# Norm sums by a matrix of ones, roots of whole rows, and buffers of its own for the second feed-forward unit

## The reference

```
def rms_norm(x, g):
    return x * rsqrt(mean(x*x, axis=-1) + 1e-6) * g
for l in range(2):                                   # first model
    mixed = mixer_l(rms_norm(h, norm_mix_pre[l])) @ w_out[l]       # recurrence / window attention, memory attention
    h = h + rms_norm(mixed, norm_mix_post[l])
    f = (silu(g) * u) @ w_ffn_out[l]                 # g, u = halves of rms_norm(h, norm_ffn_pre[l]) @ w_ffn_in[l]
    h = h + rms_norm(f, norm_ffn_post[l])
    if l == 0:
        kv = rms_norm(h, norm_kv) @ w_kv_shared
# second model: x + position, modulated norm, mLSTM and Fourier mixer, w_out_2,
# x = x + gate1 * rmsnorm(y); router on 16 experts; x + gate2 * rmsnorm(moe)
```

## Time and profile before

| what | value |
|---|---|
| median of 3 runs | 1950.71 us |
| lowest, highest | 1950.61, 1956.45 us |
| span of the profiled execution, first to last instruction | 1947.3 us |
| own time of that execution | not recorded beside its span |
| mean granted TensorE clock | 0.950 |
| TensorE busy | 1814.3 us |
| VectorE busy | 1216.2 us |
| ScalarE busy | 896.1 us |

### The profile page before, as it was taken

How to read it: one execution, slowest core, us unless ns; L and a number is a source line. 1 busy time by engine, 2 the same in 40 slices (tenths; PEclk the granted TensorE clock), 3 DMA queues, 4 the chain that set the end, 5 groups by cost and what they waited for, 6 DMA issues and landing times.

```text
span 1947.3 us, 25641 instructions
## 1 busy us (share of the span) xinstructions
PE 1814.3 (93%) x9201; PEld 1507.9 (77%) x9201; DVE 1216.2 (62%) x2170; ACT 896.1 (46%) x1452; POOL 125.7 (6%) x137
## 2 busy tenths in 40 slices
PE   7997999999999997899999999799987989999997
PEld 7875788888887865678888888678576878888885
DVE  3554668887323656456865532564575479889888
ACT  3446443222213445543223221342383368888885
POOL 1000000000000000000110000120000210110102
PEclk8898999999999998999999999799998879999999
DMA  4223225455333124024655423330011359999995
GB/s 150 87 76 115 87 64 142 134 145 147 107 96 96 44 65 184 23 65 137 182 159 149 119 93 97 112 89 22 21 67 66 108 222 377 395 385 370 386 372 187
DMA packets 203854, 289.32 MB, mean 149 GB/s; under 512 B 12332, under 2 KB 150548, under 8 KB 203636
## 3 DMA queue, kind: packets, MB, share of 16 engines
q1 hardware_dynamic: 188788, 239.56, 36.9%
q0 software_dynamic: 11920, 36.48, 6.1%
q10 hardware_dynamic: 3056, 12.06, 1.6%
HBM read 271.77 MB, written 21.53 MB: 151 GB/s over the span
## 4 chain that ended last, share of the span: by engine, by line
PE 85%; DVE 7%; ACT 6%; issue 1%; DMA 1%; POOL 0%; DVEq 0%; ACTq 0%; POOLq 0%
PE bank L200 23%; PE bank L202 23%; PE bank L201 23%; PE bank L69 11%; PE bank L654 2%; DVE weights_low L227 1%; PE bank L2195 1%; ACT weights_high L221 1%; DVE tmp L69 1%; DVE z_and_u L69 1%; DVE ring L69 1%; PE bank L1651 1%; ACT spare L69 1%; PE bank L2544 1%; PE bank L272 1%
## 5 line engine op out<-in xcount | busy, mean ns | idle before, releaser
L227 DVE TENSOR_TENSOR weights_low<-ring,weights_high 128x1024 fp32r<-128x1024 f32 x202 | 246.7, 1223 | 395.3 <-ACT weights_high L221 394.8
L200 PE MATMUL bank<-XH,weights_high 128*128 128x512 f32 x1056 | 423.2, 401 | 17.8 <-DVE weights_low L227 6.5
L202 PE MATMUL bank<-XH,weights_low 128*128 128x512 f32 x1056 | 415.6, 394 | 0.0
L201 PE MATMUL bank<-XL,weights_high 128*128 128x512 f32 x1056 | 415.2, 393 | 0.0
L221 ACT CAST weights_high<-ring 128x1024 fp32r<-128x1024 f32 x202 | 211.1, 1047 | 432.6 <-PE bank L202 422.8
L200 PEld LDWEIGHTS bank<-XH,weights_high 128*128 128x128 f32 x1056 | 200.8, 190 | 63.0 <-DVE weights_low L227 9.6
L202 PEld LDWEIGHTS bank<-XH,weights_low 128*128 128x128 f32 x1056 | 200.7, 190 | 43.4
L201 PEld LDWEIGHTS bank<-XL,weights_high 128*128 128x128 f32 x1056 | 201.1, 190 | 40.3 <-issue 0.5
L2235 DVE TENSOR_TENSOR XL<-ring,XH 128x1024 fp32r<-128x1024 f32 x144 | 169.8, 1219 | 11.7 <-ACT XH L2229 11.7
L2229 ACT CAST XH<-ring 128x1024 fp32r<-128x1024 f32 x144 | 145.2, 1048 | 0.6 <-PE bank L202 0.6
L69 DVE SCALAR_TENSOR_TENSOR squares<-ring,c_silu,squares 128x128 f32<-128x128 f32 x384 | 135.2, 352 | 13.6
(11 more groups left out here) (506 smaller groups left out, 3263.2 us busy)
## 6 DMA issues: line engine op xcount, KB each, us to landing
ring<-in_w_ffn_in SPq DMA_DIRECT2D x88, 512.0 KB, 4.7
ring<-in_w_gate SPq DMA_DIRECT2D x72, 512.0 KB, 5.4
ring<-in_w_up SPq DMA_DIRECT2D x72, 512.0 KB, 7.3
ring<-in_w_down SPq DMA_DIRECT2D x72, 512.0 KB, 5.9
ring<-in_w_ada POOLq DMA_DIRECT2D x48, 512.0 KB, 4.7
ring<-in_w_ffn_out SPq DMA_DIRECT2D x44, 512.0 KB, 3.6
ring<-in_w_out SPq DMA_DIRECT2D x24, 512.0 KB, 3.6
slot_output<-expert_out SPq DMA_DIRECT2D x18, 512.0 KB, 6.7
```

Source lines behind the costliest of these rows:

```text
L200: PE.matmul(out_ap, w_h, x_h, start=first, stop=False, skip_group_check=True)
L201: PE.matmul(out_ap, w_h, x_l, start=False, stop=False, skip_group_check=True)
L202: return PE.matmul(out_ap, w_l, x_h, start=False, stop=last, skip_group_check=True)
L227: V.tensor_tensor(wl[:, s, :], ring[s][:, :], wh[:, s, :].bitcast(F32), ALU.subtract).then_inc(split_done.sem, 1)
```

## The change

In words:

- `rows_root`: the three parts are each one product of the whole 128x128 matrix of ones with 128x512 squares, so every partition of bank 0 holds the sum of each token. Root (ScalarE) and reciprocal (VectorE) work on 128x512 and write `rstd_t`. `spread_passes` is not called there any more, nor is the copy of the spread root. The running total moves to `spare[:, 1]`. After a feed-forward the floor lies in it already, so that all squares of chunks 0 to 5 are added to it, one add more. The low halves of the next stage's weights are split earlier: half 0 ahead of the adds, half 1 ahead of the sums.
- A class `Transition` takes over the chunks with products (before both feed-forwards and before the shared keys and values). The low products of chunk k - 1 come after the high products of chunk k; of the last two chunks they come at the end, both for s = 0, then both for s = 1. The pre-norm's sums are one product with the matrix of ones per chunk (per token as before with `by_token`, ahead of the shared keys and values).
- Its root, ahead of the feed-forwards, is of 128x512 straight into `rstd_t`, and a floor of 128x512 is put in `spare[:, 1]`.
- The second feed-forward unit's weights (`Early`) are loaded to ring[2] and ring[3] before the mixer output's stream, and split in buffers of their own beside its fourth unit (first layer) or its third (second layer). The loads for the modulation that use the same ring buffers (0, 1 and 20, 21) come after. The third unit's halves are filled while the second's products run.
- The slots' counts are kept per slot; the attention probabilities of the first layer get a scope of their own that closes earlier.

The diff, cut to its core:

```diff
@@ rows_root
-            base, used, total = chunk_done.n - (KC - 1), used_done.n, tmp[:, 1, :]
-            squares = (sq[:, 0, :], sq[:, 1, :], tmp[:, 0, :], spare[:, 1, :])
+            base, used, total = chunk_done.n - (KC - 1), used_done.n, spare[:, 1, :]
+            squares = (sq[:, 0, :], sq[:, 1, :], tmp[:, 0, :], tmp[:, 1, :])
             V.wait_ge(chunk_done.sem, base + 1)
             m0 = vec.do(V.tensor_copy, kept, bank[0][:, :])
             if next_src:
                 load_half(next_src, 0, 0)
                 split_high(0)
+                split_low(0)
...
+                if c == 0 and floor:
+                    added[c] = vec.do(V.tensor_tensor, total, total, squares[0], ALU.add, after=[squared[0]])
...
             if next_src:
-                split_low(0)
                 load_half(next_src, 0, 1)
                 split_high(1)
+                split_low(1)
...
-                pe.need(ready)
-                for t in range(TT):
-                    tok = pe.do(PE.matmul, bank[0][:, t:t + 1], part[:, t * P:(t + 1) * P], ones[:, 0:1],
-                                start=n + t == 0, stop=n == 2, skip_group_check=True)
...
+                tok = pe.do(PE.matmul, bank[0][:, :], ones[:, :], part, start=n == 0, stop=n == 2, after=[ready])
+            bias = {} if floor else {"bias": epsilon[:, 0:1]}
+            t = act.do(S.activation, rstd_t[:, :], bank[0][:, :], ACT.Sqrt, scale=1.0 / D, after=[tok], **bias)
             bank_free[0] = [t]
-            t = vec.do(V.reciprocal, roots[:, 0, :], roots[:, 0, :], after=[t])
...
-            return spread_passes(0, 0, t)
+            return vec.do(V.reciprocal, rstd_t[:, :], rstd_t[:, :], after=[t])
@@ class Transition(Residual), first_unit
+                for k in range(1, KC):
+                    add(k)
+                    highs(k)
+                    square(k)
+                    if k < last:
+                        scale(k + 1)
+                    lows(k)
+                    PE.wait_ge(act.line.sem, high[k][1])
+                    for s in range(2):
+                        one_pass(s, wh, XH, k)
+                        one_pass(s, wl, XH, k)
+                    if k < last:
+                        PE.wait_ge(vec.line.sem, low[k - 1][1])
+                        for s in range(2):
+                            one_pass(s, wh, XL, k - 1)
+                    sums(k - 1)
+                for s in range(2):
+                    for k in (last - 1, last):
+                        pe.need(low[k])
+                        done = one_pass(s, wh, XL, k, stop=k == last)
+                    done.then_inc(used_done.sem, 1)
+                slots_used(0, 1)
+                sums(last)
@@ class Transition, sums and root
+                        summed[k] = pe.do(PE.matmul, bank[2][:, :], ones[:, :], squares[k % 3], start=k == 0, stop=k == last,
+                                          skip_group_check=True)
...
+                t = act.do(S.activation, rstd_t[:, :], bank[2][:, :], ACT.Sqrt, scale=1.0 / D, bias=epsilon[:, 0:1],
+                           after=[self.summed])
+                self.rooted = vec.do(V.reciprocal, rstd_t[:, :], rstd_t[:, :], after=[t])
+                floor = vec.do(V.tensor_scalar, spare[:, 1, :], bank[2][:, :], EPS / P, EPS * EPS * D / P, ALU.mult, ALU.add,
+                               after=[t])
@@ class Early
+            def load(self, *after):
+                sp.need(*after)
+                for s in range(2):
+                    ap, view = self.src(self.unit, s)
+                    load(sp, landed[2 + s], view(ring[2 + s][:, :]), ap)
+            def split(self, s, *after):
+                act.need(*after)
+                S.wait_ge(landed[2 + s].sem, landed[2 + s].n)
+                S.copy(self.high[:, s, :], ring[2 + s][:, :]).then_inc(self.high_line.sem, 1)
...
@@ stream
+                    elif early and i == 1:
+                        PE.wait_ge(early.split_line.sem, s + 1)
+                        products(i, s, False, early).then_inc(used_done.sem, 1)
...
                             for both in range(2):
+                                if early:
+                                    open_half(src, both, 2)
                                 evacuate(0, both, used_done.n - 2)
@@ the first layer's mixer output
+            if i == 3:
+                early.split(s, used_done.now())
         load(pool, tables_landed, con[:, P:], I["constants"][:, P:], after=[used_done.now()])
         pool.need(used_done.now())
+        early = Early("first_ffn", ffn_src(0), 1, unit_high, unit_low)
+        early.load(used_done.now())
+        rooted = mix_out(I["w_out"][0], ffn_src(0), row_order, row_ready, row_part)
+        G.wait_ge(early.split_line.sem, 2)
         modulation_load(0)
         modulation_load(1)
@@ the second layer's mixer output
+        early.load(used_done.now(), (ada_summed, ada_sums[19]))
+        def split_early(i, s):
+            if i == 2:
+                early.split(s, used_done.now())
+        root_table()
+        rooted = mix_out(I["w_out"][1], ffn_src(1), row_order, row_ready, split_early)
+        G.wait_ge(early.split_line.sem, 2)
+        modulation_load(20)
+        modulation_load(21)
```

More of the change, by code:

```diff
@@ L288, in opener, with stream @@
             return lambda s: open_half(src, s)
-        def stream(units, src, products, evacuate=None, side=None, then=None, fused=None, beside=None, paired=None):
+        def stream(units, src, products, evacuate=None, side=None, then=None, fused=None, beside=None, paired=None, early=None):
             pending = []
@@ L379, in columns_products, with products @@
         def columns_products(n, xh, xl, to=0, ready=None):
-            def products(i, s, first):
-                w_h = wh[:, s, :].rearrange("p (k n) -> p k n", k=KC)
-                w_l = wl[:, s, :].rearrange("p (k n) -> p k n", k=KC)
+            def products(i, s, first, halves=None):
+                high, low = (halves.high, halves.low) if halves else (wh, wl)
+                w_h = high[:, s, :].rearrange("p (k n) -> p k n", k=KC)
+                w_l = low[:, s, :].rearrange("p (k n) -> p k n", k=KC)
                 b = to + 4 * (i % 2) + s
@@ L393, in columns_products, with token_products @@
             return products
-        def token_products(tiles, xh, xl, to=0, between=None):
+        def token_products(tiles, xh, xl, to=0, between=None, early=None):
             for a in range((tiles + 1) // 2):
                 pe.need(*bank_free[to + a])
-            PE.wait_ge(split_done.sem, used_done.n + 2)
+            if early:
+                PE.wait_ge(early.split_line.sem, 2)
+            else:
+                wait_slots(0, 1)
+            w_h, w_l = (early.high, early.low) if early else (wh, wl)
             for m in range(tiles):
@@ L409, in token_products @@
             last.then_inc(used_done.sem, 2)
-            used_done.n += 2
+            if early:
+                used_done.n += 2
+            else:
+                slots_used(0, 1)
         def rows_products(units, xh, xl, ready=None, order=None, tokens=None, between=None):
@@ L573, in rows_root @@
             for n, (part, ready) in enumerate(parts):
-                pe.need(ready)
-                for t in range(TT):
-                    tok = pe.do(PE.matmul, bank[0][:, t:t + 1], part[:, t * P:(t + 1) * P], ones[:, 0:1],
-                                start=n + t == 0, stop=n == 2, skip_group_check=True)
[L578 to L582, removed]
-                           after=[tok])
-                t = act.do(S.activation, roots[:, 0, :], roots[:, 0, :], ACT.Sqrt, after=[t])
@@ L635, in sum_tokens @@
                             summed[j] = token_sums(square[j], False)
-                    elif not self.router:
-                        pe.need(squared[j])
-                        summed[j] = token_sums(square[j], j == 0)
                     else:
@@ L1460, in program @@
         row_ready = {c: outputs_done[5] for c in range(KC)}
[L1461 removed]
+        unit_high, unit_low = (QL[:, 4 * n:4 * n + 4, :].rearrange("p c t -> p (c t)").rearrange("p (s n) -> p s n", s=2)
+                               for n in range(2))
+        early = Early("second_ffn", ffn_src(1), 1, unit_high, unit_low)
+        early.load(used_done.now(), (ada_summed, ada_sums[19]))
[7 more added lines that the diff above has]
+        modulation_load(21)
         b_ctx.close()
```

251 lines of the change are left out of this document (136 added, 115 removed).

## The result

The change made the kernel slower. Median of five runs 1964.22 us (1962.08 to 1970.54) against 1950.71 us (1948.33 to 1956.45, five runs): ratio 1.007, 95% interval 1.0044 to 1.0095. The forecast was 1948.4 us, range 1939 to 1958. The profiled execution took 1962.08 us with a span of 1960.4 us; the span before was 1947.3 us, so 13.1 us are to be found. The runs of one kernel often fall in two groups some 6 us apart (after: 1962.1 to 1964.2, and 1970.1 to 1970.5), so small differences are read from the traces and not from the medians.

A forecast was written before the change was run, and what follows sets the result against it. TensorE, busy 93% of the span, was taken as the bound, so its waits and slow stretches count. Closings 5X - 7.5, chunks +1.0, second units -7.8 gave -2.3 us at X = 2.4: 1948.4 us, range 1939 to 1958.

The forecast's parts named there:

- The term 5X: Five closing chains: X is one uncovered 128x512 reciprocal on VectorE, taken as 2.4 us, bounds 0.69 and 4.2.
- 18.15 + 5X: Five closings, first full-width sum to first scale: their summed us after the change, against 25.7 before.
- 5X - 7.5: Five closings: net change in us; costs 4.5 at X = 2.4, breaks even at X = 1.5.
- rival (b): Five closings: slower reciprocal becomes their bound, over 0.3% slower from X = 4.04; chance 0.23 for X from 3.2 on.
- at 3.3: Case of a slower reciprocal in the closings, X = 3.3 us: +2.2 us, kernel at 1952.9.
- Buffers taken from closed scopes: no time: Memory for the new buffers: listed among the parts of the change that cost nothing.
- forecast of -2.3: Whole kernel: net change in us, 5X - 14.3 at X = 2.4.
- The closing of the first mixer output: First closing: early split delays copy and adds, sums to scale 4.35 + X, or 0.9 more if the clock falls.
- The chunks: Products over the chunks before both feed-forwards: about +0.15 us each, called 0.3; with the third stretch +1.0, from -1 to +3.
- +0.7 after the first feed-forward: Chunk stretch there: first half's weights released 0.7 us later, value weights' casts and subtracts exposed, +0.7 us.
- The second unit: Second feed-forward unit: wait, spread, late third unit and low clock all go, 3.9 us each, -7.8 for both.
- rival (c): After the chunk stretch: clock falls all the same whatever the products' width, +0.9 us, 1951.6; chance 0.10.

The follow-up runs named there:

- e1: The changed kernel with one unused 128x4 tile put back where the small floor tile stood, so later tiles keep their old addresses: 1954.74 us, ratio 1.002.
- e2: The kernel before with its floor kept in a fourth column group of the roots tile, so all later tiles lie 32 bytes lower: 1959.38 us, ratio 1.0046.
- e4: The kernel before with an unused 128x4 tile ahead of each feed-forward's two hidden tiles, moving only these 32 bytes up: 1955.01 us, ratio 1.0023.
- e9: The kernel before with 64 bytes of unused memory ahead of each feed-forward's two hidden tiles: 1954.05 us, ratio 1.0012.
- e5: e1 without the early buffers, the second feed-forward unit's weights sharing the first one's slots again: 1957.36 us, ratio 1.0021.
- e7: e3 with the pre-norm's sums and root by token again in the chunks before the feed-forwards, early buffers kept: 1960.67 us, ratio 1.003.
- e8: e3 with both early splits of the first layer issued in the first half of the fourth unit: 1945.53 us, ratio 0.9963.
- e10: e8 with 64 bytes ahead of x_high_b and x_low_b, so that these begin at a multiple of 128: 1944.47 us, ratio 0.9953.
- e3: e1 with the small sums, roots, reciprocals and spreading products back in the closings, all else of the change kept: 1944.38 us, ratio 0.9969.

## Why the prediction was wrong

**The term 5X.** The step that failed is "I take the slope of the reciprocal's own rows, the nearest thing there is: 0.16 + 512 x 0.0044 = 2.4 us". It was 3.353 us. The form of the sum held: from the first full-width sum to the first scale it said 18.15 + 5X, 34.9 us at the measured X, and the trace has 6.96, 6.87, 6.96, 6.87 and 6.96, together 34.6 (before: 25.7). From the start of the last product the five are 10.1 us longer, where 5X - 7.5 at 3.353 gives 9.3 and the forecast had 4.5. Small durations that differ by 14 ns can't carry a slope over 512 columns: the rows gave 4.4 ns a column and the full width has 6.2, a difference of only 5 ns between one column and four. The two bounds (0.69 and 4.2 us) were honest, and the middle of them, 2.45, would have been no better. This was rival (b) in its mechanism, the reciprocal uncovered five times, at a size below the 4.04 us where it decides alone: for "at 3.3" the prediction had 1952.9 us, and e1, the change with its tiles in place, came at 1954.74. The Trainium skill's page VectorE: DVE Perf Modes (First, the fixed hardware budget), which speaks of iterative divide steps with a repeat count of 8, pointed to the right side: the estimate from it was 4.3 us, the row has 3.35.

**"Buffers taken from closed scopes: no time", and the tile that goes.** This step failed too, and it is why the result lies outside the range. I priced the instructions of the change and not its memory layout; the removal of `root_floor` stood nowhere in the sum. It cost 7.0 us in the output streams (e1, e2 and e4 each show it), nearly the 7.8 that the second unit brought. With it undone (e1, 1954.74 us) the kernel lies inside the range. Of the 15.4 us between the forecast of -2.3 and the 13.1 in the traces, the closings make 5.6 and the output streams 7.0. The placement theory is shown: with the hidden tiles at a multiple of 128 the row of the tile has 119.1 us between its first and last start (before, e1), at 96 or 32 past one 122.6 (after, e4), at 64 past one 120.3 (e9).

**The closing of the first mixer output** was priced at 4.35 + X for late adds. The adds were not late: TensorE waited 1.27 us before the first sum instead. The early low half on VectorE (229.97) held up the kept copy (231.12, before 229.01), and ScalarE's squares begin with that copy. The size was about right: 0.95 more than the other closings was forecast, and 1.17 measured (8.62 against 7.45; without the early split, in e5, this closing too has 7.45).

**The chunks,** forecast +0.3 for the two stretches before the feed-forwards, took 1.2 more (0.6 in e1). A reading in it was off: the clock was low until 246.4, not 247.6, and stood at 1.00 for 17 us before it fell, not 14. The +0.7 after the first feed-forward isn't seen apart from the layer around it.

**The second unit: -7.8, measured -7.8** (3.95 and 3.87). The size held and rival (c), the clock falling all the same, did not occur. But the parts don't add as I added them, so the agreement is in part luck. e5 and e7 each undo one side: the buffers are worth 1.07 and the wide sums and root 2.64, together 3.71 in the first feed-forward. The new weights' buffers also cost some 0.3 us each by their own placement, as e8 and e10 show for the second. The small sums alone, to which I put down the fall of the clock, don't bring it: it is there, 3.4 us at 0.50 in both feed-forwards, in the four kernels that have both the small sums and the wait for the second unit's weights (before, e2, e4, e9), and in neither e5 nor e7, which have one each. But these four are also the only ones with the old order of products over the chunks, which no run tried by itself, so the cause stays open. The late third unit, which I put down to shared buffers, is not late in e5 either.

**What stays open.** The mixers and the rest differ by +2.7 us in these two traces. Over the twelve traces the time to the first closing alone varies from 232.3 to 239.5 us. The three longest (e2, e7 and e10, 239.1 to 239.5) had a mean granted clock of 0.89 in it, the shortest (e3, 232.3) 0.93, and e3 and e7 run the same program there. So I read nothing from the 2.7.

## What to carry to other kernels

Before you replace a small operation and a spread by one operation on the full width, find the full-width duration of that very operation, because here a slope over a few columns didn't give it; where it is uncovered, each repetition costs its whole length. Add the memory layout to the list of what a change does: a tile removed or added shifts those declared behind it, and here 32 bytes cost nearly as much as the best part of the change brought. Keep the parts apart: the change's units and pre-norms with the old closings and the old placement (e3) made 0.9969 of the time before, where the whole made 1.007.

## What the runs showed of the hardware

- A reciprocal of 128x512 fp32 took 3.353 us on VectorE, the same within 1 ns seven times; a tensor-tensor of that shape takes 0.68.
- fp32r products of 128x512 started 0.227 us apart with the moving tile at a multiple of 128 bytes (before, e1), 0.2335 at 32 or 96 past one (e4; after, e2), and 0.229 at 64 past one (e9): hidden tiles, 1.00 clock, no gaps.
- The weights' tile counts as well: with `x_low_b` as weights and the moving tiles unmoved, 0.2333 at 64 past a multiple of 128 (e8) and 0.2274 at one (e10). In the first feed-forward the weights in `next_unit_high` and `next_unit_low` begin 64 past one in the kernel after and 96 past one in e1, and the products are 0.2334 and 0.2341 us apart.
- 64 past a multiple has no single price: 0.229 for the hidden tiles (e9) and for `x_low_b` as weights in e7, 0.2333 for `x_low_b` as weights in e8 and for `x_high_b` before. What decides between the two is not shown.
